# Differential attention on one Trainium2 core: the order of transposes, scores and sums on TensorE

## The chip, the core and the metric

The kernel runs on one core of a Trainium2 chip. The metric is the device time of one execution in microseconds (us), the median of several runs. The profile shows one execution: TensorE (PE; its weight loads are PEld), VectorE (DVE), ScalarE (ACT), GpSimd (POOL) and SyncE (SP, which issues transfers). The engines run side by side, each through its own instructions in the order of the program, and wait for each other by semaphores only.

## What is computed

Two transformer blocks one after the other, on 1024 tokens of width 1024. The change touches one stage of the second block, attention with two softmaxes per head: 4 heads, head width 64 for each of the two parts, values of width 128, 1024 queries and 1280 keys (256 of a context and the 1024 tokens). Cut to what matters:

```python
def diff_attend(q, k, v, lam):
    s = jnp.einsum('bqhmd,bkhmd->bhmqk', q, k, preferred_element_type=jnp.float32)
    a = jax.nn.softmax(s * (1.0 / math.sqrt(ATTN_HEAD_DIM)), axis=-1)
    a = a[:, :, 0] - lam * a[:, :, 1]
    return jnp.einsum('bhqk,bkhe->bqhe', a.astype(v.dtype), v)

def head_out(o, subln_g, lam_init):
    b, t = o.shape[:2]
    return (rmsnorm(o, subln_g) * (1.0 - lam_init)).reshape(b, t, ATTN_V_W)
```

The index m is the part (0 or 1). After this stage come the output projection and a mixture of experts, which take most of the rest of the kernel together with the same steps of the first block.

## The kernel before

The kernel is a chain of stages, each a block in which every engine has its own program and at whose end all meet. The stage here is `differential_attention` (line 2600). It goes through G = 32 groups: head h = g // 8, query tile t = g % 8 of 128 queries. All of TensorE's results go to 8 banks of PSUM, each of 128 partitions x 512 numbers. Banks 0 to 2 hold the scores of part 0 (128 queries x 1280 keys), banks 3 to 5 those of part 1, banks 6 and 7 the transposed probabilities, and bank 7 also the sums. For each group:

- `scores(g, i)` (line 2657, matmuls on lines 2672 and 2676): six matmuls for part i. They wait until ScalarE has read the part's scores of the group before (`exped[i]`).
- `bias(g, i)` on VectorE (line 2743, the reduction on 2746): the negated maximum of each row of scores.
- `exp(g, i)` on ScalarE (line 2792, on 2800): the exponentials with their row sums. The results lie in `e[g % 2]`.
- `combine(g)` on VectorE (line 2748; reciprocals on 2753 and 2755, the ratio on 2756, the combination on 2758): part 0 minus the scaled part 1, in place.
- `turn(g, r)` on TensorE (line 2680, transposes on 2692), three parts by r: the ten key tiles are turned so that keys lie on partitions. `GROUPS` gives the tiles of a part and `BANK` its bank. Part 0 (tiles 0 to 3, bank 6) waits for `combined`, part 1 (tiles 4 to 7, bank 7) for `kept`, part 2 (tiles 8 and 9, bank 6 again) for the first copy out of bank 6.
- `move(g, r)` on ScalarE (line 2803, on 2808): the copy of one part from its bank to `at_[g % 2]` in SBUF.
- `sums(g)` on TensorE (line 2696, matmuls on 2701): 20 recorded loads and matmuls against the values, into bank 7. They wait for all three copies of the group.
- `keep(g)` on VectorE (line 2761, on 2765): the sums times the reciprocal of part 0, out of bank 7. `square(g)` on ScalarE (2812) and `norm(g)` on GpSimd (2865) end the group.

The loops are written out by hand, and their order is fixed on each engine. VectorE, per g: `bias(g + 1, 0)`, `combine(g)`, `bias(g + 1, 1)`, `keep(g - 1)`. ScalarE, per g: `exp(g + 1, 0)`, `exp(g + 1, 1)`, `square(g - 2)`, the three moves of g. TensorE, per g (lines 2710 to 2719): `scores(g + 1, 1)`, `sums(g - 1)`, `turn(g, 0)`, `scores(g + 2, 0)`, `turn(g, 1)`, `turn(g, 2)`. GpSimd first splits the queries and keys of heads 1 to 3 into high and low parts (`split`, subtractions on lines 2852 and 2860), then normalizes group after group. SyncE issues four loads of 512 KB for the next stage. In the trace the scores' operands are called upper_split_qk, the probabilities arena, and the copies' targets arena or upper_tail.

Of the kernel before, what the change touches and what calls it, by code (L numbers as in the profile page):

```python
# [49 lines left out]
NK2 = SA // P  # L50
# [110 lines left out]
def rounded(ap):  # L161

    return ap.bitcast(F32R)
# [2434 lines left out]
def differential_attention(core, m):  # L2600
# [14 lines left out]
    combined, turned, moved, summed, kept, steps, gained, squared, normed, pool_steps = map(sem, (  # L2615
        "combined", "turned", "moved", "summed", "kept", "steps", "gained", "squared", "normed", "pool_steps"))
    e, at_ = m["e2"], m["a2"]
    at = m["free_too"]

    def take(*shape):  # L2620
        nonlocal at
        n = int(np.prod(shape))
        at += n
        return core.place(at - n, *shape)
# [1 line left out]
    G = NH2 * NT  # L2626
    nb, den, inv, ratio = take(4), take(4), take(4), take(4)
    gain, junk, ss, rs = take(P), take(P), take(G), take(G)
    GROUPS = ((0, 4), (4, 8), (8, NK2))
    BANK = (6, 7, 6)  # L2630
    FOLD = float(HD2) ** -0.5
    full = ps[:].rearrange("p a b -> p (a b)")
    rows = [full[:, 3 * i * HALF:3 * i * HALF + SA] for i in range(2)]
# [3 lines left out]
    with nc.Block() as block:  # L2637
        @block.sync
        def _(sp):
            for i in range(2):  # L2640
                sp.wait_ge(k_low[i], 1)
            sp.wait_ge(k_split[NH2 - 1], 2)
            for k in range(4):
                sp.dma_start(m["wo2"][k], core.ins["w_out2_k"][:, k, :]).then_inc(m["wo2_loaded"], 16)
            sp.wait_ge(m["wo2_loaded"], 16 * 4)

        @block.tensor
        def _(pe):
            def turn_v(h):
                i = (h + 1) % 2  # L2650
                if h >= 2:
                    pe.wait_ge(v_moved[h - 2], 2)
                for t in range(NK2):
                    ins = pe.transpose(rows[i][:, t * P:(t + 1) * P], v1[:, h, t * P:(t + 1) * P], core.col("ident"))
                ins.then_inc(v_turned[h], 1)

            def scores(g, i):
                h, t = where(g)
                x, cols = 2 * (h % HEADS) + i, slice(t * P, (t + 1) * P)
                if g:  # L2660
                    pe.wait_ge(exped[i], g)
                if t == 0:
                    if h == 0:
                        pe.wait_ge(v_moved[3 - i], 2)
                        pe.wait_ge(k_low[i], 1)
                        pe.wait_ge(q_copied[i], 2)
                    else:
                        pe.wait_ge(k_split[h], 2)
                        pe.wait_ge(q_split[h], 2)
                for c, wd in enumerate((HALF, HALF, CTX)):  # L2670
                    keys = slice(c * HALF, c * HALF + wd)
                    pe.matmul(ps[:, 3 * i + c, 0:wd], rounded(qa[:, x, cols]), rounded(ka[:, x, keys]),
                              start=True, stop=False, skip_group_check=True)
                for c, wd in enumerate((HALF, HALF, CTX)):
                    keys = slice(c * HALF, c * HALF + wd)
                    t = pe.matmul(ps[:, 3 * i + c, 0:wd], rounded(ql[:, x, cols]), rounded(ka[:, x, keys]),
                                  start=False, stop=True, skip_group_check=True)
                t.then_inc(scored[i], 1)

            def turn(g, r):  # L2680
                lo, hi = GROUPS[r]
                if r == 0:
                    pe.wait_ge(combined, g + 1)
                    if g:
                        pe.wait_ge(moved, 3 * g)
                elif r == 1:
                    if g:
                        pe.wait_ge(kept, g)
                else:
                    pe.wait_ge(moved, 3 * g + 1)  # L2690
                for t in range(lo, hi):
                    ins = pe.transpose(ps[:, BANK[r], (t - lo) * P:(t - lo + 1) * P],
                                       e[g % 2][:, 1, t * P:(t + 1) * P], core.col("ident"))
                ins.then_inc(turned, 1)

            def sums(g):
                h, _ = where(g)
                pe.wait_ge(moved, 3 * g + 3)
                for t in range(NK2):
                    own = at_[g % 2][t // 8]  # L2700
                    ins = pe.matmul(ps[:, 7, 0:P], own[:, t % 8, :], vt[t // 8][:, t % 8, h * P:(h + 1) * P],
                                    start=(t == 0), stop=(t == NK2 - 1), skip_group_check=True)
                ins.then_inc(summed, 1)

            for h in range(NH2):
                turn_v(h)
            scores(0, 0)
            scores(0, 1)
            scores(1, 0)
            for g in range(G):  # L2710
                if g + 1 < G:
                    scores(g + 1, 1)
                if g:
                    sums(g - 1)
                turn(g, 0)
                if g + 2 < G:
                    scores(g + 2, 0)
                turn(g, 1)
                turn(g, 2)
            sums(G - 1)  # L2720

        def move_v(eng, copy, h):
            i = (h + 1) % 2
            eng.wait_ge(v_turned[h], 1)
            for lo, hi, dst in ((0, 8, vt[0]), (8, NK2, vt[1])):
                copy(dst[:, :, h * P:(h + 1) * P],
                     rows[i][:, lo * P:hi * P].rearrange("p (a b) -> p a b", b=P)).then_inc(v_moved[h], 1)
# [57 lines left out]
        @block.scalar  # L2785
        def _(a):
            def high(i):
                a.activation(rounded(ka[here[i], i, :]), k[here[i], 0, :], ACT.Copy).then_inc(k_high[i], 1)
                a.activation(rounded(qa[here[i], i, :]), q[here[i], 0, :], ACT.Copy, scale=FOLD)\
                 .then_inc(q_high[i], 1)  # L2790

            def exp(g, i):
                x = 2 * (g % 2) + i
                a.wait_ge(biased[i], g + 1)
                if g >= 2:
                    if i == 0:
                        a.wait_ge(combined, g - 1)
                    else:
                        a.wait_ge(turned, 3 * (g - 1))
                a.activation(e[g % 2][:, i, :], rows[i], ACT.Exp, bias=nb[:, x:x + 1],  # L2800
                             accum_out=den[:, x:x + 1]).then_inc(exped[i], 1)

            def move(g, r):
                lo, hi = GROUPS[r]
                a.wait_ge(turned, 3 * g + r + 1)
                if g >= 2:
                    a.wait_ge(summed, g - 1)
                a.activation(at_[g % 2][r // 2][:, lo % 8:lo % 8 + hi - lo, :],
                             ps[:, BANK[r], 0:(hi - lo) * P].rearrange("p (a b) -> p a b", b=P), ACT.Copy)\
                 .then_inc(moved, 1)  # L2810

            def square(g):
                h, i = where(g)
                a.wait_ge(kept, g + 1)
                if g:
                    a.wait_ge(squared, g)
                a.activation(junk, o[:, h, i * P:(i + 1) * P], ACT.Square, accum_out=ss[:, g:g + 1])\
                 .then_inc(squared, 1)

            high(0)  # L2820
            high(1)
            copy = lambda dst, src: a.activation(dst, src, ACT.Copy)
            for h in (0, 2, 3):
                move_v(a, copy, h)
            exp(0, 0)
            exp(0, 1)
            for g in range(G):
                if g + 1 < G:
                    exp(g + 1, 0)
                    exp(g + 1, 1)  # L2830
                if g >= 2:
                    square(g - 2)
                for r in range(3):
                    move(g, r)
            square(G - 2)
            square(G - 1)
# [723 lines left out]
def build(nc, ins, out):  # L3560

    with ExitStack() as ctx:
# [150 lines left out]
        with ExitStack() as kind:  # L3713
# [18 lines left out]
        m["wo2_loaded"], m["wo2_rest"], m["rows_loaded"] = map(core.semaphore, (  # L3732
            "wo2_loaded", "wo2_rest", "rows_loaded"))
        run(differential_attention, m)
        kind.close()
        del core.regions[tail]
# [154 lines left out]
```

## Time and profile before

| | before |
|---|---|
| runs, us | 3062.36, 3063.38, 3066.44 |
| median, us | 3063.38 |
| the profiled execution, us | 3064.91 |
| its span in the profile, us | 3062.8 |
| granted TensorE clock, mean | 0.97 |
| TensorE matmul, busy us (share of the span) | 2854.3 (93%) |
| VectorE, busy us | 2088.0 (68%) |
| ScalarE, busy us | 1580.2 (52%) |
| GpSimd, busy us | 491.6 (16%) |

The profile is one execution on the core. All times in it are us from the start of the span unless marked ns. PE busy is the time in which a matmul was in flight; since matmuls overlap, the starts of the weight loads (PEld) show better when TensorE went on to the next. A row of the timeline merges like instructions that follow on one another; what stands in brackets is how long the engine was idle before it, and who released it. The clock is given as a share of full speed: 1.00 is 2.4 GHz and 0.50 is 1.2 GHz.

### The profile page before, as it was taken

What the parts mean: (1) busy time and instruction counts of PE and PEld (TensorE: products, weight loads), DVE (VectorE), ACT (ScalarE), POOL (GpSimd) and SP (SyncE); (2) the same over time, 40 slices, a digit from 0 to 9 for tenths busy, and PEclk for the clock granted to TensorE, in tenths of its full rate; (3) what the DMA queues carried; (4) which work ended last, traced back from release to release, by engine and by line L of the source; (5) the groups of instructions that cost most, each with busy time, mean ns of one, the idle gap of its engine ahead of it and who ended that gap; (6) DMA issues with size and microseconds to landing.
All of it is one profiled execution on the core that took longest, in us unless ns stands there. A gap on an engine that the chain in (4) does not pass through costs nothing. (4 is left out here: it accounts for less than half of the span.)

```text
span 3062.8 us, 38625 instructions
## 1 busy us (share of the span) xinstructions
PE 2854.3 (93%) x14112; PEld 2295.7 (75%) x14112; DVE 2088.0 (68%) x2213; ACT 1580.2 (52%) x1951; POOL 491.6 (16%) x501
## 2 busy tenths in 40 slices
PE   6998998999999999999998989998989579999998
PEld 4884466788877778888886878887877468888886
DVE  6988454332327788888886743317866679999997
ACT  4111565532212277787785531116663168887885
POOL 0004500000000011111112312009643100000001
PEclk9998999999999999999999999999999789999999
DMA  7112332643227476996215511100005669999997
GB/s 274 48 34 76 121 87 67 186 154 144 97 83 282 164 277 246 407 413 236 92 58 206 177 59 51 52 14 24 6 1 200 241 256 409 408 400 399 398 396 264
DMA packets 144569, 574.68 MB, mean 188 GB/s; under 512 B 18520, under 2 KB 41840, under 8 KB 104496
## 3 DMA queue, kind: packets, MB, share of 16 engines
q1 hardware_dynamic: 116560, 486.05, 41.8%
q0 software_dynamic: 15696, 57.15, 5.6%
q10 hardware_dynamic: 12176, 29.63, 2.7%
q8 instruction: 88, 1.44, 0.2%
q14 instruction: 49, 0.40, 0.0%
HBM read 584.99 MB, written 82.17 MB: 218 GB/s over the span
## 5 line engine op out<-in xcount | busy, mean ns | idle before, releaser
L2023 DVE TENSOR_TENSOR upper_split<-arena,upper_split 128x2048 fp32r<-128x2048 f32 x185 | 413.0, 2285 | 67.4 <-ACT upper_split L1970 65.7
L3505 DVE TENSOR_TENSOR upper_split_experts<-arena,upper_split_experts 128x1024 fp32r<-128x1024 f32 x288 | 337.6, 1221 | 33.5 <-ACT upper_split_experts L3449 33.4
L1970 ACT ACTIVATE upper_split<-arena 128x2048 fp32r<-128x2048 f32 x184 | 339.5, 1911 | 7.5 <-PE banks L177 6.6
L3449 ACT ACTIVATE upper_split_experts<-arena 128x1024 fp32r<-128x1024 f32 x288 | 288.5, 1053 | 83.9 <-PE banks L177 83.9
L175 PE MATMUL banks<-upper_split_experts 128*128 128x512 f32 x768 | 303.2, 395 | 6.1 <-DVE upper_split_experts L3505 3.6
L175 PE MATMUL banks<-upper_split 128*128 128x512 f32 x744 | 297.4, 400 | 4.5 <-PEq L1622 2.1
L177 PE MATMUL banks<-upper_split_experts 128*128 128x512 f32 x768 | 300.5, 391 | 0.0
L176 PE MATMUL banks<-upper_split_experts 128*128 128x512 f32 x768 | 300.0, 391 | 0.0
L177 PE MATMUL banks<-upper_split 128*128 128x512 f32 x744 | 291.7, 392 | 0.0
L176 PE MATMUL banks<-upper_split 128*128 128x512 f32 x744 | 291.0, 391 | 0.0
L175 PEld LDWEIGHTS banks<-upper_split_experts 128*128 128x128 f32 x768 | 145.1, 189 | 35.9 <-issue 4.0
L175 PE MATMUL banks<-upper_split_xn 128*128 128x512 f32 (+1 forms) x448 | 169.7, 379 | 2.3 <-DVE upper_split_xn L2306 1.6
L176 PE MATMUL banks<-upper_split_xn 128*128 128x512 f32 (+1 forms) x448 | 169.2, 378 | 0.0
L177 PE MATMUL banks<-upper_split_xn 128*128 128x512 f32 (+1 forms) x448 | 168.5, 376 | 0.0
L177 PEld LDWEIGHTS banks<-upper_split_experts 128*128 128x128 f32 x768 | 144.8, 189 | 30.6
L176 PEld LDWEIGHTS banks<-upper_split_experts 128*128 128x128 f32 x768 | 145.2, 189 | 29.4
L175 PEld LDWEIGHTS banks<-upper_split 128*128 128x128 f32 x744 | 140.4, 189 | 33.1 <-issue 3.3
L177 PEld LDWEIGHTS banks<-upper_split 128*128 128x128 f32 x744 | 140.5, 189 | 30.7
L176 PEld LDWEIGHTS banks<-upper_split 128*128 128x128 f32 x744 | 140.7, 189 | 27.9
L249 DVE SCALAR_TENSOR_TENSOR arena<-arena 128x1024 f32<-128x1024 f32 x120 | 153.7, 1322 | 1.7
L1296 DVE TENSOR_TENSOR upper_latent<-upper_latent,arena 128x512 f32<-128x512 f32 x48 | 33.3, 693 | 175.7 <-ACT upper_latent L1248 175.7
L175 PE MATMUL banks<-upper_split_h,upper_split_gates 128*128 128x512 f32 x384 | 149.5, 389 | 1.1 <-DVE upper_split_gates L1268 1.1
(486 smaller groups left out, 6308.2 us busy)
## 6 DMA issues: line engine op xcount, KB each, us to landing
arena<-in_exp_up_k SPq DMA_DIRECT2D x124, 1024.0 KB
arena<-in_gate_up SPq DMA_DIRECT2D x96, 1024.0 KB, 9.1
arena<-in_exp_down_k SPq DMA_DIRECT2D x62, 1024.0 KB
arena<-in_down SPq DMA_DIRECT2D x48, 1024.0 KB, 8.0
upper_middle<-in_gate_up SPq DMA_DIRECT2D x32, 1024.0 KB, 8.6
upper_middle<-in_down SPq DMA_DIRECT2D x16, 1024.0 KB, 8.1
y<-arena POOLq DMA_DIRECT2D x31, 512.0 KB, 4.1
arena<-in_merge_w SPq DMA_DIRECT2D x8, 1536.0 KB, 10.3
```

The lines of the kernel that those rows point to most:

```text
L175: pe.matmul(out, rounded(lh), rounded(rh), start=first, stop=False, skip_group_check=True)
L176: pe.matmul(out, rounded(lh), rounded(rl), start=False, stop=False, skip_group_check=True)
L177: return pe.matmul(out, rounded(ll), rounded(rh), start=False, stop=last, skip_group_check=True)
L249: t = v.scalar_tensor_tensor(acc, src, weight, acc, ALU.mult, ALU.add)
L1296: v.tensor_tensor(part[min(b, 1)], sg[done % 4], y[t % 2][:, b, here], ALU.mult).then_inc(steps, 1)
L1970: a.activation(rounded(high[s]), raw[s], ACT.Copy).then_inc(high_made[up], 1)
L2023: v.tensor_tensor(rounded(low[s]), raw[s], plain(high[s]), ALU.subtract).then_inc(low_made[up], 1)
L3449: a.activation(rounded(high[n % RING][:, half]), raw[n % RAW][:, half], ACT.Copy).then_inc(high_made, 1)
L3505: v.tensor_tensor(rounded(low[n % RING][:, half]), raw[n % RAW][:, half], plain(high[n % RING][:, half]), ALU.subtract).then_inc(low_made, 1)
```

## The change

`sums(g - 1)` is placed behind `turn(g, 0)` and `scores(g + 2, 0)`. The transposes of tiles 8 and 9 come second, into bank 6, with the wait for the first copy out of it. Those of tiles 4 to 7 come third, into bank 7, with the wait for `kept`. ScalarE's copies follow the new order of the parts, and each tile goes to the same place in SBUF as before. VectorE's and GpSimd's programs are as they were.

```diff
--- before.py
+++ after.py
@@ -2626,8 +2626,8 @@
     G = NH2 * NT
     nb, den, inv, ratio = take(4), take(4), take(4), take(4)
     gain, junk, ss, rs = take(P), take(P), take(G), take(G)
-    GROUPS = ((0, 4), (4, 8), (8, NK2))
-    BANK = (6, 7, 6)
+    GROUPS = ((0, 4), (8, NK2), (4, 8))
+    BANK = (6, 6, 7)
     FOLD = float(HD2) ** -0.5
     full = ps[:].rearrange("p a b -> p (a b)")
     rows = [full[:, 3 * i * HALF:3 * i * HALF + SA] for i in range(2)]
@@ -2684,10 +2684,9 @@
                     if g:
                         pe.wait_ge(moved, 3 * g)
                 elif r == 1:
-                    if g:
-                        pe.wait_ge(kept, g)
-                else:
                     pe.wait_ge(moved, 3 * g + 1)
+                elif g:
+                    pe.wait_ge(kept, g)
                 for t in range(lo, hi):
                     ins = pe.transpose(ps[:, BANK[r], (t - lo) * P:(t - lo + 1) * P],
                                        e[g % 2][:, 1, t * P:(t + 1) * P], core.col("ident"))
@@ -2710,11 +2709,11 @@
             for g in range(G):
                 if g + 1 < G:
                     scores(g + 1, 1)
-                if g:
-                    sums(g - 1)
                 turn(g, 0)
                 if g + 2 < G:
                     scores(g + 2, 0)
+                if g:
+                    sums(g - 1)
                 turn(g, 1)
                 turn(g, 2)
             sums(G - 1)
@@ -2805,7 +2804,7 @@
                 a.wait_ge(turned, 3 * g + r + 1)
                 if g >= 2:
                     a.wait_ge(summed, g - 1)
-                a.activation(at_[g % 2][r // 2][:, lo % 8:lo % 8 + hi - lo, :],
+                a.activation(at_[g % 2][lo // 8][:, lo % 8:lo % 8 + hi - lo, :],
                              ps[:, BANK[r], 0:(hi - lo) * P].rearrange("p (a b) -> p a b", b=P), ACT.Copy)\
                  .then_inc(moved, 1)
```

## Rows read from the trace of the kernel before

**Rows 1.** The page, part 1: busy us, share of the span, instructions.

```profile
PE 2854.3 (93%) x14112; PEld 2295.7 (75%) x14112; DVE 2088.0 (68%) x2213; ACT 1580.2 (52%) x1951; POOL 491.6 (16%) x501
```

**Rows 2.** Table by stretch, the stage whole; the first line names the columns.

```profile
core 0: us, PE busy (x) PEld busy (x) DVE busy (x) ACT busy (x) POOL busy (x), PEclk, DMA share, GB/s
...
2076.92:2294.24 217.32, 193.56 (x1344) 173.02 (x1344) 169.68 (x224) 142.72 (x287) 148.99 (x163) 0.98 0.03 11
```

**Rows 3.** Timeline, weight loads, two groups: start, us, engine, line, operation [idle before].

```profile
2189.97 1.87 PEld L2701 LDWEIGHTS banks<-upper_middle,upper_tail 128*128 128x128 f32 x16
...
2192.65 0.54 PEld L2672 LDWEIGHTS banks<-upper_split_qk 128*128 128x128 f32 x3
...
2193.82 0.47 PEld L2692 LDWEIGHTS banks<-arena 128*128 128x128 f32 x4
...
2195.58 0.20 PEld L2692 LDWEIGHTS banks<-arena 128*128 128x128 f32 x2 [1.28 <-ACT arena L2808]
...
2196.91 1.87 PEld L2701 LDWEIGHTS banks<-upper_middle,arena 128*128 128x128 f32 x16
...
2199.15 0.47 PEld L2692 LDWEIGHTS banks<-arena 128*128 128x128 f32 x4
...
2202.66 1.43 PEld L2701 LDWEIGHTS banks<-upper_middle,upper_tail 128*128 128x128 f32 x12
```

**Rows 4.** Timeline, ScalarE, the same two groups.

```profile
2193.34 1.33 ACT L2800 ACTIVATE arena<-banks,upper_tail 128x1280 f32<-128x1280 f32 x1 [2.01 <-DVE upper_tail L2746]
...
2194.95 1.07 ACT L2808 ACTIVATE arena<-banks 128x512 f32<-128x512 f32 x2
```

**Rows 5.** Timeline, VectorE, the same two groups.

```profile
2194.14 1.49 DVE L2746 TENSOR_REDUCE upper_tail<-banks 128x1 f32<-128x1280 f32 x1 [0.58 <-PE banks L2676]
...
2195.54 0.15 DVE L2753 RECIPROCAL upper_tail<-upper_tail 128x1 f32<-128x1 f32 x1
...
2196.10 1.55 DVE L2758 SCALAR_TENSOR_TENSOR arena<-arena,upper_tail 128x1280 f32<-128x1280 f32 x1
...
2199.46 0.35 DVE L2765 TENSOR_SCALAR arena<-banks,upper_tail 128x128 f32<-128x128 f32 x1 [0.41 <-PE banks L2701]
```

**Rows 6.** Timeline, weight loads and VectorE, first and last groups of the stage.

```profile
2092.31 1.87 PEld L2701 LDWEIGHTS banks<-upper_middle,arena 128*128 128x128 f32 x16
...
2092.78 2.30 DVE L2758 SCALAR_TENSOR_TENSOR arena<-arena,upper_tail 128x1280 f32<-128x1280 f32 x1
...
2095.13 0.42 PEld L2692 LDWEIGHTS banks<-arena 128*128 128x128 f32 x4 [0.51 <-DVE arena L2758]
...
2095.52 0.53 PEld L2672 LDWEIGHTS banks<-upper_split_qk 128*128 128x128 f32 x3
...
2273.01 1.87 PEld L2701 LDWEIGHTS banks<-upper_middle,arena 128*128 128x128 f32 x16
...
2293.89 0.35 DVE L2765 TENSOR_SCALAR arena<-banks,upper_tail 128x128 f32<-128x128 f32 x1 [4.21 <-PE banks L2701]
```

**Rows 7.** Groups by line in the stage; count | busy us, mean ns; then one line (min/median/max).

```profile
L2758 DVE SCALAR_TENSOR_TENSOR arena<-arena,upper_tail 128x1280 f32<-128x1280 f32 x32 | 54.4, 1699 | 1.1
...
L2852 POOL TENSOR_TENSOR upper_split_qk<-arena,upper_split_qk 64x1280 fp32r<-64x1280 f32 x6 | 17.5, 2922 | 0.5
...
L2758 DVE SCALAR_TENSOR_TENSOR arena<-arena,upper_tail x32: 1550/1553/2355, 2086.0 to 2284.1; 128x1280 f32<-128x1280 f32 x32
```

**Rows 8.** Timeline, GpSimd, the end of its splitting.

```profile
2152.53 2.18 POOL L2843 CAST upper_split_qk<-upper_split_qk 64x1024 fp32r<-64x1024 f32 x1
```

**Rows 9.** Table by stretch, columns as in rows 2, start of the stage.

```profile
2083.65:2087.07 3.42, 1.66 (x8) 0.98 (x6) 3.04 (x5) 1.77 (x4) 3.33 (x2) 1.00 0.00 0
...
2087.07:2090.48 3.41, 2.84 (x10) 2.45 (x11) 1.91 (x2) 1.46 (x3) 3.20 (x4) 0.50 0.00 0
```

**Rows 10.** Timeline, weight loads, start of the stage.

```profile
2082.46 0.53 PEld L2672 LDWEIGHTS banks<-upper_split_qk 128*128 128x128 f32 x3 [1.76 <-ACT arena L2800]
...
2087.64 0.71 PEld L2692 LDWEIGHTS banks<-arena 128*128 128x128 f32 x4 [2.47 <-DVE arena L2758]
```

## The prediction, made before the changed kernel was run

> **What bounds the kernel now.** I read the page first: TensorE is busy for 93% of the whole span [rows 1], so on average it is the bound, and an average says nothing of one stage. The stretch table of the stage that the diff touches (first score to last sum, 217.3 us) shows 193.6 us of TensorE and 169.7 us of VectorE [rows 2]: neither is full. The stage treats 32 groups. Its timeline repeats every two of them: the sums of group 15 start at 2189.97, those of group 17 at 2202.66, so a pair takes 12.69 us and a group 6.35 [rows 3].
>
> In one pair TensorE idles once for long: 1.28 us at 2195.58, ahead of the last two transposes, until ScalarE has copied the first four out of bank 6 [rows 3]. That copy (2194.95, two copies in the row) was late because it stands behind both exponentials [rows 4]. Everything else on TensorE is back to back: without that wait a group is (12.69 - 1.28) / 2 = 5.70 us. Of these the sums take 2.24 (2196.91 to 2199.15) and each of the two score blocks 1.17 (2192.65 to 2193.82) [rows 3], which leaves 1.12 for the ten transposes, 0.11 each. VectorE waits too, 0.58 us for scores and 0.41 for sums in the rows shown [rows 5]. So it has slack as the orders stand now.
>
> **Part by part.** All instructions stay, so nothing is removed or added. Moved are (a) `sums(g - 1)`, 20 matmuls, behind `turn(g, 0)` and `scores(g + 2, 0)`; (b) the two transposes of key tiles 8 and 9 to second place; (c) the four of tiles 4 to 7 to bank 7 and last place, behind the wait for `kept`; ScalarE's copies follow the same order. No DMA and no SyncE or GpSimd instruction is moved or passed.
>
> (b) The two transposes still need the first copy out of bank 6, but now 2.24 us of sums stand ahead of that wait. In the new order that copy ends before the sums do (worked out below), so the 1.28 us per pair go.
>
> (c) The last four transposes wait for `keep(g - 1)`, which now follows directly on the sums. From the first load of the sums to the start of `keep` it takes 2.55 us (2196.91 to 2199.46), `keep` itself 0.35 [rows 3, 5]; with 0.04 for the signal (an estimate, next to the 0.05 below) they can start 2.94 after the sums did, and TensorE has work for 2.24 + 0.22. That is 0.48 us idle in each group. Taken alone, a group would be 6.18 us, slightly under the 6.35 of now.
>
> (a) is what decides. VectorE's program is not changed: per group `bias(g+1, 0)`, `combine(g)`, `bias(g+1, 1)`, `keep(g-1)`, in that order, and it cannot pass a waiting `keep`. Behind `keep(g-1)` are queued `bias(g+2, 0)` and `combine(g+1)`. On TensorE, `sums(g)` now stands behind `turn(g+1, 0)`, which waits for `combine(g+1)`, and behind `scores(g+3, 0)`. So the sums of one group wait, through five instructions of VectorE, for the sums of the group before. Today this ring does not exist: sums stand ahead of the transposes that wait for `combine`. The ring, step by step:
> - sums, first load to start of `keep`: 2.55 [rows 3, 5]
> - `keep`: 0.35 [rows 5]
> - `bias` to the first reciprocal: 1.40 (2194.14 to 2195.54) [rows 5]
> - reciprocals and ratio to the start of the combination: 0.56 (to 2196.10) [rows 5]
> - the combination: 1.55 [rows 5]
> - signal to TensorE 0.05 (2092.78 + 2.30 = 2095.08, transposes at 2095.13) and four transposes 0.39 (to 2095.52) [rows 6]
> - the score block: 1.17 [rows 3]
>
> Sum 8.02 us a group against 6.35. Checking who else could be later, counted from the start of the sums: the combination before ended at -(1.17 + 0.39 + 0.05) = -1.61; `bias(g+1, 1)` follows and takes 1.5 (the row at 2194.14) [rows 5], from the start of its exponential to that of the first copy are 1.61 (2193.34 to 2194.95) [rows 4], the copy is 0.6, so it ends at about 2.1, under 2.24; the other score block runs from 3.4 to 4.5; TensorE then idles until 6.45, about 1.9 us. The ring is the longest chain and VectorE and TensorE wait in turn: about 2.3 us of 8.02 TensorE is idle.
>
> Entry: `sums(0)` starts at 2092.31 now [rows 6]. After the change it waits for the combination of group 1, which ends at 2095.08 either way, then 0.05 + 0.39 + 1.17: 2096.69, that is +4.4. Middle: from `sums(0)` to `sums(28)` (2273.01) are 28 groups, 180.7 us now [rows 6]; then 28 x 8.02 = 224.6, +43.9. Exit: the last three groups have no further scores to serve and take 21.2 us now (2273.01 to 2294.24) [rows 6]; the waits there are only exchanged, so 0, between -1.7 and +1.7.
>
> One term is not in 8.02. While GpSimd splits keys and queries the combination takes longer: 1699 ns in the mean of 32 against 1550, 4.8 us in all, longest 2355 [rows 5, 7]. 0.75 of it is in the entry. The splitting ends at 2154.7 [rows 8]; about 9 groups of now share the other 4.0, about 7 of the new ones lie in the same time, and now each such delay is on the ring: +3.2, between 0 (GpSimd out of step) and 7 x 0.80 = 5.6.
>
> Sum: 4.4 + 43.9 + 3.2 = +51.5. For the clock (next part) I add 1.7, one slow stretch, against 0 to 7: +53.2. The profiled execution is 3062.8 us and 3064.9 with what lies around it; its run is 1.5 above the median of the three. So 3064.9 + 53.2 - 1.5 = 3116.6; I say 3117.
>
> **Rivals.**
> *The clock falls.* TensorE works 5.7 of 8.0 us with a gap of 1.9 in each group. In this trace it idled 1.76 us and went on at full rate, and after 2.47 us four weight loads took 0.71, not the 0.42 of 2095.13 [rows 6, 10]; the clock granted around that gap fell from full to half (2.4 to 1.2 GHz) for 3.4 us, after a stretch with 1.66 us of work in 3.42 [rows 9]. The new gap is nearer to the first. A combination of 2.3 us makes it 2.7. A slow stretch of 3.4 us on the ring costs at most half, 1.7: four of them in GpSimd's part +7, one in every group +48, 3164.
>
> *The combination is blocked for whole instructions.* Rows: GpSimd's subtraction takes 2922 ns, and no combination is more than 0.80 us longer than its shortest [rows 7]. If each of the 7 waited a whole one, that is +20 in place of 3.2: 3133. The Trainium skill, "SBUF — State Buffer", section "SBUF: two separate sides", says so: one of GpSimd and a VectorE operation with two SBUF inputs holds the shared ports to its end. By that rule the time would be 3133; the trace shows 0.80 at most, so I trust it little.
>
> *Not slower: TensorE sets the pace.* If VectorE's order did not close the ring, a group would be 6.18 us: 28 x 6.18 = 173.0, +4.4 entry, 3.3 less than now: 3060. With (c)'s wait hidden as well, 5.70 a group, 16.7 less: 3047. It decides from the point at which `bias(g+2, 0)` can start before `keep(g-1)`: its scores are done some 2.2 us before `keep`. VectorE would have to serve them out of order; in the rows each `keep` stands where the program has it, at 2199.46 after a wait of 0.41 [rows 5].
>
> **How the numbers follow.** Forecast (ring, few slow stretches) 0.76; clock beyond 7 us 0.14; blocked combinations 0.03; TensorE's pace 0.04 (3060 and 3047, half each); the rest, a mis-sized term beyond the bounds, 0.03. The forecast's own bounds: -1.7 exit, -3.2 combinations, -1.7 clock, -2.5 if `keep` hands over at 0.26: 3107. Upward 2.4 + 5.3 + 1.7 and 0.1 a group (2.8): 3129. To leave out no more than 2 in 10 the range goes on into the clock's case: 3107 to 3135. A measurement can tell about 0.2% (6 us) from no change. Faster 0.02, same 0.02, slower 0.96.
>
> **What would show it.** In the profile after: sums 8.0 us apart in every group, no more pairs; VectorE waiting for the sums ahead of `keep` about 2.9 us, and not for scores ahead of the first `bias`; TensorE waiting for the combination about 1.9 us ahead of the first transposes and for `keep` about 0.5; no wait for the first copy; all other stages unchanged. I am wrong if sums stand 6.2 apart (no ring), or if the granted clock of the stage falls well below 0.98.

## The result, and the profile after

| | before | after |
|---|---|---|
| median of the runs, us | 3063.72 (4 runs, 3062.36 to 3066.44) | 3114.96 (4 runs, 3114.60 to 3116.24) |
| ratio to before | | 1.0168 (1.0157 to 1.0180) |
| profiled execution, us | 3064.91 | 3116.24 |
| its span, us | 3062.8 | 3114.3 |
| the stage, first score to end of the last `keep`, us | 217.3 | 269.7 |
| TensorE busy in the stage, us | 193.6 | 203.3 |
| VectorE busy in the stage, us | 169.7 | 168.5 |
| a group in the quiet part of the stage, us | 6.35 | 7.92 |

The change costs 51.2 us, 1.7%. The prediction was 3117, with 3107 to 3135 as the range. The span is 51.5 us longer, and the stage ends 51.5 us later (2345.78 in place of 2294.24), so all of it is in the stage. (The first score came 0.9 us earlier, at 2076.05 in place of 2076.92; counted from there the stage is 52.4 longer.) The stretch table of after, over the stage and over one group:

```profile
core 0: us, PE busy (x) PEld busy (x) DVE busy (x) ACT busy (x) POOL busy (x), PEclk, DMA share, GB/s
2076.05:2345.80 269.75, 203.29 (x1344) 174.19 (x1344) 168.50 (x224) 148.15 (x287) 134.16 (x164) 0.97 0.02 9
2199.62:2207.54 7.92, 6.08 (x44) 5.23 (x43) 5.10 (x7) 4.60 (x10) 1.81 (x4) 1.00 0.00 0
```

To be read against rows 2: 52 us more, of which VectorE has none and TensorE 10. Both wait more. What one group looks like now stands in the timeline of TensorE's weight loads (line 2691 holds the transposes, 2700 the sums):

```profile
2198.07 0.42 PEld L2691 LDWEIGHTS banks<-arena 128*128 128x128 f32 x4 [1.93 <-DVE arena L2757]
...
2199.62 1.87 PEld L2700 LDWEIGHTS banks<-upper_middle,arena 128*128 128x128 f32 x16
...
2201.41 0.53 PEld L2700 LDWEIGHTS banks<-arena,upper_tail 128*128 128x128 f32 x4
...
2201.85 0.25 PEld L2691 LDWEIGHTS banks<-arena 128*128 128x128 f32 x2
...
2202.57 0.42 PEld L2691 LDWEIGHTS banks<-arena 128*128 128x128 f32 x4 [0.46 <-DVE arena L2764]
...
2202.96 0.53 PEld L2672 LDWEIGHTS banks<-upper_split_qk 128*128 128x128 f32 x3
...
2205.99 0.42 PEld L2691 LDWEIGHTS banks<-arena 128*128 128x128 f32 x4 [1.93 <-DVE arena L2757]
...
2206.38 0.53 PEld L2672 LDWEIGHTS banks<-upper_split_qk 128*128 128x128 f32 x3
...
2207.54 1.87 PEld L2700 LDWEIGHTS banks<-upper_middle,upper_tail 128*128 128x128 f32 x16
```

From one start of the sums (2199.62) to the next (2207.54) are 7.92 us, in every group alike; the pairs of [rows 3] are gone. TensorE waits twice: 1.93 us for the combination ahead of the first four transposes, and 0.46 for `keep` ahead of the last four. It no longer waits for the first copy out of bank 6: the two transposes at 2201.85 follow the sums at once. VectorE in the same group (2745 the reduction, 2757 the combination, 2764 `keep`):

```profile
2202.17 0.35 DVE L2764 TENSOR_SCALAR arena<-banks,upper_tail 128x128 f32<-128x128 f32 x1 [2.75 <-PE banks L2700]
2202.43 1.48 DVE L2745 TENSOR_REDUCE upper_tail<-banks 128x1 f32<-128x1280 f32 x1
2203.83 0.15 DVE L2752 RECIPROCAL upper_tail<-upper_tail 128x1 f32<-128x1 f32 x1
2204.39 1.55 DVE L2757 SCALAR_TENSOR_TENSOR arena<-arena,upper_tail 128x1280 f32<-128x1280 f32 x1
2205.86 1.48 DVE L2745 TENSOR_REDUCE upper_tail<-banks 128x1 f32<-128x1280 f32 x1
```

VectorE stands idle for 2.75 us ahead of `keep`, and from then on nothing of the ring waits: `keep`, the reduction of the scores that had long been ready, the reciprocal, the combination; then TensorE's transposes at 2205.99, scores and sums. In [rows 5] `keep` waited 0.41 and the reduction 0.58 for scores; in the other group of the pair the reduction waited 1.26. Over the whole stage VectorE now waits 92.8 us for the sums. The two ends of the middle part (first sums, the 29th sums, the last `keep`), which answer to [rows 6]:

```profile
2096.49 1.87 PEld L2700 LDWEIGHTS banks<-upper_middle,arena 128*128 128x128 f32 x16
...
2326.29 1.87 PEld L2700 LDWEIGHTS banks<-upper_middle,arena 128*128 128x128 f32 x16
...
2345.43 0.35 DVE L2764 TENSOR_SCALAR arena<-banks,upper_tail 128x128 f32<-128x128 f32 x1 [3.94 <-PE banks L2700]
```

### The profile page after: what moved, and what is told of

It reads as the page before. It is cut to its first block and busy times, and to the rows that moved or that the text cites. A ratio compares the mean times of both kernels' runs of the same rounds, so it can differ in the third digit from the quotient of the medians.

```text
span 3114.3 us, 38625 instructions
## 1 busy us (share of the span) xinstructions
PE 2862.0 (92%) x14112; PEld 2297.3 (74%) x14112; DVE 2088.0 (67%) x2213; ACT 1586.0 (51%) x1951; POOL 476.0 (15%) x501
## 5 line engine op out<-in xcount | busy, mean ns | idle before, releaser
L175 PE MATMUL banks<-upper_split_xn 128*128 128x512 f32 (+1 forms) x448 | 169.7, 379 | 2.3 <-DVE upper_split_xn L2306 1.6
```

Of the source, the lines that this page charges most:

```text
L175: pe.matmul(out, rounded(lh), rounded(rh), start=first, stop=False, skip_group_check=True)
```

## Experiments

All kernels ran with the kernel before on the same chip; medians of before were between 3061.8 and 3063.7. "A group" is the distance from one start of the sums to the next in the quiet part of the stage, behind GpSimd's splitting.

| kernel | median, us | ratio to before (interval) | a group, us |
|---|---|---|---|
| after | 3114.96 | 1.0168 (1.0157 to 1.0180) | 7.92 |
| e3_sums_moved, part (a) alone | 3114.67 | 1.0162 (1.0145 to 1.0179) | 7.92 |
| e2_order_of_parts, (b) and (c) alone | 3071.53 | 1.0026 (1.0017 to 1.0036) | 6.56 |
| e4_sums_half_way | 3110.25 | 1.0151 (1.0134 to 1.0168) | 7.67 |
| e1_bias_first | 3078.48 | 1.0043 (1.0031 to 1.0056) | 6.77 |
| e5_second_reduction | 3121.45 | 1.0192 (1.0177 to 1.0207) | 8.18 |
| e11_no_gain | 3116.99 | 1.0171 (1.0154 to 1.0189) | 7.92 |
| e7_no_split | 3106.98 | 1.0137 (1.0122 to 1.0152) | 7.92 |
| e8_copy_between | 3055.79 | 0.9978 (0.9968 to 0.9987) | 6.09 |
| e9_square_last | 3058.34 | 0.9980 (0.9972 to 0.9989) | 6.10 |

The theory is the prediction's: a ring through six instructions of VectorE (`keep`, the reduction, two reciprocals, the ratio, the combination) and three steps of TensorE (four transposes, a score block, the sums), closed by part (a). The rivals are that the new order of the parts carries the loss, that the amount of work on VectorE does, or that TensorE has its own reasons.

### Which part of the change does it

Part (a) alone, on the kernel before:

```diff
-                if g:
-                    sums(g - 1)
                 turn(g, 0)
                 if g + 2 < G:
                     scores(g + 2, 0)
+                if g:
+                    sums(g - 1)
```

> Part (a) alone: the sums behind the first transposes and the scores, the parts and banks as before. Ring theory: the ring is closed by (a) alone, and the waits of (b) and (c) lie inside TensorE's 2.3 us of slack: 7.92 us a group, 3115 within 2 us of the changed kernel. Rival that (b) and (c) carry a part: between 3064 and 3110.

Measured 3114.67 and 7.92 us a group. The parts keep their old order here, and the waits look different inside the group (timeline of the weight loads; 2701 are the sums, 2692 transposes):

```profile
2198.37 1.87 PEld L2701 LDWEIGHTS banks<-upper_middle,arena 128*128 128x128 f32 x16
...
2201.32 0.64 PEld L2692 LDWEIGHTS banks<-arena 128*128 128x128 f32 x6 [0.64 <-DVE arena L2765]
...
2204.74 0.42 PEld L2692 LDWEIGHTS banks<-arena 128*128 128x128 f32 x4 [1.71 <-DVE arena L2758]
...
2206.28 1.87 PEld L2701 LDWEIGHTS banks<-upper_middle,upper_tail 128*128 128x128 f32 x16
```

Six transposes wait 0.64 us for `keep`, the first four 1.71 for the combination, and the distance of the sums is the same 7.92. How the slack is cut up makes no difference; (a) is the whole loss.

Parts (b) and (c) alone are the changed kernel with the sums put back ahead of `turn(g, 0)`:

> Parts (b) and (c) alone: the sums stand where they stood before, the two transposes of tiles 8 and 9 come second into bank 6, the four of tiles 4 to 7 last into bank 7. Ring theory: no ring, since the sums are ahead of the transposes that wait for the combination; the wait for the first copy out of bank 6 stays and has 0.45 us of transposes less ahead of it, only in every second group: up to 0.2 us a group more than before, 3064 to 3071. Rival that the new order of the parts (the wait for keep) carries the loss: 3080 or more.

Measured 3071.5, 8.6 us above the kernel before and half a microsecond above the range that was expected; that only every second group would be longer did not come true. Groups of 6.87 and 6.25 us take turns, 13.12 a pair against 12.69: 0.21 us a group more. The wait for the first copy is now there in both groups of a pair (0.70 and 1.32 us), since the four transposes that used to stand ahead of it stand behind it. So (b) and (c) are a small loss by themselves, which the ring hides once it is closed.

### Does the ring have the members that the prediction gave it?

The sums moved by half the way, behind the transposes but ahead of the scores:

```diff
                 turn(g, 0)
-                if g + 2 < G:
-                    scores(g + 2, 0)
                 if g:
                     sums(g - 1)
+                if g + 2 < G:
+                    scores(g + 2, 0)
```

> The changed kernel with the sums moved past the first transposes only; scores(g+2, 0) stand behind the sums again. Ring theory: the ring now runs sums 2.24, score block with its last results 1.17 + 0.32, reduction 1.40, reciprocals and ratio 0.56, combination 1.55, signal 0.05, four transposes 0.39 = 7.68 us a group, 0.24 less than 7.92: 28 x 0.24 = 6.7 less, about 3108. Rival that the scores between transposes and sums are simply 1.17 us of the ring that leave it: 6.75 a group, 3082. Rival without a ring: 3064.

```profile
2200.98 0.42 PEld L2691 LDWEIGHTS banks<-arena 128*128 128x128 f32 x4 [2.12 <-DVE arena L2757]
...
2201.37 1.86 PEld L2700 LDWEIGHTS banks<-upper_middle,arena 128*128 128x128 f32 x16
...
2208.65 0.42 PEld L2691 LDWEIGHTS banks<-arena 128*128 128x128 f32 x4 [2.12 <-DVE arena L2757]
...
2209.04 1.87 PEld L2700 LDWEIGHTS banks<-upper_middle,upper_tail 128*128 128x128 f32 x16
```

Measured 7.67 a group (2201.37 to 2209.04) where 7.68 was worked out, and 3110.25 where 3108 was. The score block did not leave the ring by changing places with the sums. It took the place of `keep`: the reduction now waits for it (0.82 us, behind a `keep` that is done).

One edit on VectorE alone, the reduction ahead of `keep`:

```diff
             bias(0, 1)
+            bias(1, 0)
             for g in range(G):
-                if g + 1 < G:
-                    bias(g + 1, 0)
                 combine(g)
                 if g + 1 < G:
                     bias(g + 1, 1)
+                if g + 2 < G:
+                    bias(g + 2, 0)
                 if g:
                     keep(g - 1)
```

> The changed kernel with one edit on VectorE alone: bias(g+2, 0) stands ahead of keep(g-1), not behind it. Ring theory: the 1.40 us of that reduction leave the ring, the combination stays on it, since it is still queued behind keep: 7.92 - 1.40 + 0.13 (the combination waits for the end of keep, 0.35, not for its hand-over, 0.26, and 0.04 of signal) = 6.65 us a group, so 1.27 x 28 = 35.6 us less than the changed kernel and one slow clock stretch fewer: about 3078, still slower than before. TensorE's-pace theory (the ring was only the reduction, as the rival in the prediction had it): 6.18 a group, about 3061. Rival that VectorE's order has nothing to do with it (the sums are late for TensorE's own sake): unchanged, 3115.

```profile
2199.68 0.42 PEld L2691 LDWEIGHTS banks<-arena 128*128 128x128 f32 x4 [0.78 <-DVE arena L2757]
...
2201.22 1.87 PEld L2700 LDWEIGHTS banks<-upper_middle,upper_tail 128*128 128x128 f32 x16
...
2204.16 0.42 PEld L2691 LDWEIGHTS banks<-arena 128*128 128x128 f32 x4 [0.47 <-DVE arena L2764]
...
2206.46 0.42 PEld L2691 LDWEIGHTS banks<-arena 128*128 128x128 f32 x4 [0.80 <-DVE arena L2757]
...
2208.00 1.87 PEld L2700 LDWEIGHTS banks<-upper_middle,arena 128*128 128x128 f32 x16
```

Measured 6.77 us a group (2201.22 to 2208.00; 6.65 expected) and 3078.5 (3078 expected). Ahead of the first transposes 0.80 us of wait are left of 1.93. 36 of the 51 us come back without touching TensorE. About 32 of them are the shorter ring (28 x 1.15); the stretch from `sums(0)` to `sums(28)` is 39.1 us shorter in the profile, which has no half-clock stretch there. The 0.12 beyond the expectation: the combination takes 1.62 us beside GpSimd, not 1.55, and the first reciprocal starts 0.46 after `keep`, not 0.39. The prediction's rival had it that without that reduction the ring would be open and a group 6.18. It is not: the combination is still behind `keep`, and the shorter ring still sets the pace. The program's order is not the only thing that holds it there: `combine(g + 1)` overwrites the reciprocals that `keep(g - 1)` reads, and waits for `kept`.

### Is it the work of VectorE, or its place?

The changed kernel with a second, unused reduction where VectorE waits for the sums:

```diff
                 v.wait_ge(scored[i], g + 1)
+                if i and g >= 2:
+                    v.tensor_reduce(spare, rows[i], AX, ALU.max, negate=True)
                 v.tensor_reduce(nb[:, x:x + 1], rows[i], AX, ALU.max, negate=True).then_inc(biased[i], 1)
```

> The changed kernel with work added on VectorE off the ring: the reduction of bias(g+1, 1) is done twice from group 2 on (once into an unused column), 1.40 us more of VectorE in 30 groups, 42 us in all. It stands between the combination and keep, where VectorE waits 2.75 us in each group. Ring theory: it fills that wait; the second exponential and the first copy come 1.4 later, the two transposes then wait until about 3.5 after the start of the sums instead of 2.2, but TensorE had slack until 6.4: 7.92 us a group, 3115 within 3 us. Rival that VectorE's work is what costs the time: 3157.

Measured 3121.45: far from 3157, but 6.5 us above the changed kernel and outside the 3 us given. A group took 8.18. GpSimd and VectorE in one group (2872 and 2873 are the last two steps of GpSimd's normalization, 2760 the combination, 2747 the added reduction, 2767 `keep`):

```profile
2205.97 0.61 POOL L2872 TENSOR_SCALAR arena<-arena,upper_tail 128x128 f32<-128x128 f32 x1
...
2206.66 0.47 POOL L2873 TENSOR_TENSOR arena<-arena,upper_tail 128x128 f32<-128x128 f32 x1
...
2206.65 1.82 DVE L2760 SCALAR_TENSOR_TENSOR arena<-arena,upper_tail 128x1280 f32<-128x1280 f32 x1
...
2208.39 1.48 DVE L2747 TENSOR_REDUCE upper_tail<-banks 128x1 f32<-128x1280 f32 x1
...
2212.61 0.35 DVE L2767 TENSOR_SCALAR arena<-banks,upper_tail 128x128 f32<-128x128 f32 x1 [1.35 <-PE banks L2701]
```

VectorE still waits 1.35 us ahead of `keep` (the added 1.40 came out of the 2.75), so the reduction is not what lengthens the group. The combination takes 1.82 us, not 1.55, in all quiet groups (1810 ns in the median of the 32), and it starts with GpSimd's multiplication by the gain, 2206.65 beside 2206.66. The squares start 1.40 us later in the group than in the changed kernel, and GpSimd's multiplication with them (4.78 after the start of the sums in place of 3.36): onto the combination. That was an observation from one profile, so the next kernel takes the multiplication away:

```diff
-                c.step(g.tensor_scalar(row, row, r, None, ALU.mult))
-                g.tensor_tensor(row, row, gain, ALU.mult).then_inc(normed, 1)
+                g.tensor_scalar(row, row, r, None, ALU.mult).then_inc(normed, 1)
```

> As e5_second_reduction, with GpSimd's last step of each group, the multiplication with the gain (0.47 us, it reads two operands out of SBUF), left out; so the gain is missing from the heads' output. In e5_second_reduction a group took 8.18 us, not 7.92, and each combination 1.81, not 1.55; it started 0.01 us before or after that multiplication. Theory that the combination waited for the end of the multiplication: with it gone the combinations take 1.55 again and a group 7.92, in spite of the second reduction: about 7 us less than e5_second_reduction, 3114. Rival that the added reduction itself lengthens the ring by 0.26: 8.18 a group stays, 3121.

```profile
2209.89 0.61 POOL L2872 TENSOR_SCALAR arena<-arena,upper_tail 128x128 f32<-128x128 f32 x1
2210.58 1.55 DVE L2760 SCALAR_TENSOR_TENSOR arena<-arena,upper_tail 128x1280 f32<-128x1280 f32 x1
```

The combination takes 1.55 us again and a group 7.92, with the second reduction in place. The median fell to 3117.0, 4.5 us less than with the multiplication where 7 were expected (its runs spread from 3112.2 to 3119.6). The times alone would not decide it: the profiled execution of e11_no_gain is the longer of the two, 3119.6 against 3117.8; the 7.92 a group does. 1.40 us of VectorE work in a group are free at this place, and 0.27 us on the ring are not.

Only in the last three groups, where no scores are left to do, does the added reduction cost time. TensorE waits 2.32 us there for the first copy in place of 0.93, and the clock is granted at half behind that wait; from `sums(28)` to the end of the stage are 22.5 us in e5_second_reduction and 23.3 in e11_no_gain, against 19.5.

### What lies between 7.92 a group and the time

28 groups of 7.92 are 221.8 us; from `sums(0)` to `sums(28)` the changed kernel took 229.8. The other 8.0 us lie in groups ahead of 2192, while GpSimd splits or catches up. The longest of these groups took 10.65 us; GpSimd, VectorE and TensorE in it:

```profile
2144.12 2.89 POOL L2851 TENSOR_TENSOR upper_split_qk<-arena,upper_split_qk 64x1280 fp32r<-64x1280 f32 x1
...
2144.98 3.38 DVE L2757 SCALAR_TENSOR_TENSOR arena<-arena,upper_tail 128x1280 f32<-128x1280 f32 x1
...
2147.10 3.89 POOL L2854 TENSOR_SCALAR arena<-arena 128x1024 f32<-128x1024 f32 x1
...
2148.41 0.42 PEld L2691 LDWEIGHTS banks<-arena 128*128 128x128 f32 x4 [3.76 <-DVE arena L2757]
```

The combination starts at 2144.98 and takes 3.38 us: GpSimd's subtraction runs to 2147.01, and from there to 2148.36 are 1.35 us, most of a combination. The 1.82 us in e5_second_reduction end as far behind the multiplication: 2207.13 to 2208.47. GpSimd's next step, 2.77 us in the kernel before, takes 3.89 and overlaps the rest. The wait of the one for the other is inside the recorded duration, not in the idle time. TensorE waited 3.76 us for it. The three stretches in which the clock was granted at half (1.2 GHz) within the middle part:

```profile
2104.47:2107.88 3.41, 3.41 (x17) 3.32 (x16) 0.02 (x1) 2.19 (x5) 3.27 (x3) 0.50 0.00 0
2121.53:2124.95 3.42, 3.42 (x15) 3.03 (x14) 1.07 (x1) 2.19 (x5) 3.28 (x3) 0.50 0.00 0
2148.84:2152.25 3.41, 3.41 (x15) 3.02 (x13) 0.92 (x1) 2.19 (x5) 3.28 (x3) 0.50 0.99 401
```

Each came after a gap on TensorE that was longer than the usual 1.93: 2.21, 2.58 and 3.76 us. Not every such gap brought one: after 2.42 us at 2094.95 and 2.20 at 2190.16 the rate stayed full. The middle one:

```profile
2121.25 0.46 PEld L2691 LDWEIGHTS banks<-arena 128*128 128x128 f32 x4 [2.58 <-DVE arena L2757]
2121.70 0.98 PEld L2672 LDWEIGHTS banks<-upper_split_qk 128*128 128x128 f32 x3
```

Three weight loads of a score block take 0.98 us in place of 0.53. In the 17 groups from 2191.70 to 2326.29, with a gap of 1.93 us each and 0.46 more, the full rate was not taken back once. In the middle part six combinations are longer than 1.6 us, by 3.3 us in all, which leaves, by difference, 4.7 for the three stretches, 1.6 each. Whether both come from GpSimd is what the next kernel asks; `split(h)` and the waits for it are left out.

> The changed kernel with GpSimd's splitting of keys and queries for heads 1 to 3 left out: all heads are scored with head 0's operands, so part of the computation is changed; GpSimd only normalizes. Theory (GpSimd in the way of the combinations, and the clock stretches that follow from it, make up all of the time beyond 7.92 a group): 28 groups at 7.92, 8.0 us less in the middle and 0.6 less ahead of it, no half-clock stretch between the first and the last sums: 3106. Theory of the prediction (3.2 us by the combinations, at most 0.80 each, the clock apart from that): 3110, the slow clock stretches staying. Rival that the long groups have another cause: 3115.

Measured 3106.98, and every group from the first to the 29th sums took 7.91 to 7.93 us, without a half-clock stretch among them. All of the 8.0 us hang on GpSimd's splitting and the catching up behind it: directly through the ring, and through the clock. How they divide between the two no run shows; both went together.

### Is the wait for the first copy what holds the kernel before back?

On the kernel before, ScalarE alone:

```diff
                 if g + 1 < G:
                     exp(g + 1, 0)
+                move(g, 0)
+                if g + 1 < G:
                     exp(g + 1, 1)
                 if g >= 2:
                     square(g - 2)
-                for r in range(3):
+                for r in range(1, 3):
                     move(g, r)
```

> The kernel before with one edit on ScalarE alone: the first copy of a group, move(g, 0), stands between exp(g+1, 0) and exp(g+1, 1), not behind both. If the 1.28 us that TensorE waits for this copy in every second group is all that holds the kernel before back, as the prediction said: the copy is taken at about 2.8 after the start of the sums in every group, the two transposes find bank 6 free, and a group takes between 5.70 (TensorE alone) and 6.0 (the second exponential starts up to 0.4 later, and the score block waits for it) instead of 6.35: 10 to 18 us less, 3046 to 3053. Rival that the wait is exchanged for another one: 3063.

ScalarE (2800 the exponential, 2808 the copies) and TensorE's loads:

```profile
2198.44 1.32 ACT L2800 ACTIVATE arena<-banks,upper_tail 128x1280 f32<-128x1280 f32 x1
...
2200.03 0.60 ACT L2808 ACTIVATE arena<-banks 128x512 f32<-128x512 f32 x1
...
2194.97 1.87 PEld L2701 LDWEIGHTS banks<-upper_middle,upper_tail 128*128 128x128 f32 x16
...
2198.80 0.69 PEld L2692 LDWEIGHTS banks<-arena 128*128 128x128 f32 x6
...
2199.90 0.53 PEld L2672 LDWEIGHTS banks<-upper_split_qk 128*128 128x128 f32 x3 [0.41 <-ACT arena L2800]
...
2201.05 1.87 PEld L2701 LDWEIGHTS banks<-upper_middle,arena 128*128 128x128 f32 x16
```

Measured 3055.8, ratio 0.9978 (0.9968 to 0.9987): faster than both kernels, though less than the 10 us expected. Six transposes go through in one run at 2198.80. In their place the next score block waits 0.41 us for the second exponential, in every group: 6.09 us a group in place of 6.35. The median is 7.7 us lower (the interval of the ratio allows 4 to 10). In the profiles 4.6 of it lie between `sums(0)` and `sums(28)` (176.1 in place of 180.7 us): 0.26 in each of the last 18 groups, while the first ten took 66.5 us in both kernels. There the long combinations add up to 9.5 us in place of 4.7, the longest 4.28. The rest of the 7.7 is not placed. The expectation had a group at 6.0 at most.

> As e8_copy_between, and the square of group g-2 behind the last copy, not ahead of the second. The other two copies come 0.3 us earlier. Theory that the second score block now waits only for the second exponential: same as e8_copy_between within 2 us; theory that the copies ahead of the sums set the pace: 0.3 us a group less, about 8 us less than it. Either way under 3055.

With the squares behind the last copy: 3058.3, ratio 0.9980 (0.9972 to 0.9989), 6.10 a group. Both kernels were expected under 3055 and are not, and the median is 2.5 us above e8_copy_between, but the intervals of the two overlap and the groups are alike. Copies that come earlier gain nothing: the copies behind the second exponential do not set the pace there.

## Why the prediction was right, point by point

- **The ring.** It closed as described, on (a) alone, and lasts 7.92 us where 8.02 was worked out. The 0.10 is the hand-over from `keep` to the reduction: 0.26 us (2202.17 to 2202.43), not the full 0.35, which stood as the lower bound. 28 x 0.10 = 2.8 us less. The prediction counted five instructions of VectorE; with both reciprocals they are six, and all their time is in the sum.
- **Entry.** `sums(0)` at 2096.49, 4.2 us later than before; 4.4 was said. Part of the agreement is luck, since the first score came 0.9 us earlier: from it to `sums(0)` are 20.4 us in place of 15.4.
- **Middle.** 229.8 us; 224.6 + 3.2 + 1.7 = 229.5 was said. The agreement is partly luck: the ring was 2.8 too long, and the clock was too small, three slow stretches (4.7) and not one (1.7).
- **GpSimd.** 3.3 us of longer combinations against 3.2. The sum held, by luck in part, since one combination makes 1.83 of it; the bound did not: "no combination is more than 0.80 us longer" was true of one profile of before. The Trainium skill, "SBUF — State Buffer", section "SBUF: two separate sides", has the two engines exclude each other for a whole instruction when VectorE reads two operands from SBUF and GpSimd reads SBUF too. The 3.38 us above and e11_no_gain agree with it, and the prediction was wrong to trust it little. What did not follow is the rival's price: few combinations meet the start of a long instruction, so the sum was 3.3 and not 20. The trace of before already spoke for whole instructions. The longest combination there:

```profile
2129.67 2.91 POOL L2852 TENSOR_TENSOR upper_split_qk<-arena,upper_split_qk 64x1280 fp32r<-64x1280 f32 x1
...
2131.57 2.35 DVE L2758 SCALAR_TENSOR_TENSOR arena<-arena,upper_tail 128x1280 f32<-128x1280 f32 x1
```

It ends 1.34 us behind the end of the subtraction (2132.58 to 2133.92). So do, by 1.34 to 1.36, seven of the nine long combinations in the middle part of before and five of the six in that of the changed kernel; the other three stand beside a multiplication by a scalar (2855, in the changed kernel 2869) and end sooner. The 0.80 was what was left of an instruction that had started 1.90 us earlier, and no bound.

- **Exit.** 19.5 us (2326.29 to 2345.78) against 21.2: -1.7, the lower bound; 0 was said. Not only the waits changed: the kernel before had a half-clock stretch here (2285.02 to 2288.44, PEclk 0.50), and the changed kernel none. The 16 loads of a group's sums took 3.36 us in it, where the changed kernel takes 1.86:

```profile
2285.29 3.36 PEld L2701 LDWEIGHTS banks<-upper_middle,arena 128*128 128x128 f32 x16 [0.71 <-ACT upper_tail L2808]
```

- **(b) and (c).** The 1.28 us per pair went, 0.48 (measured 0.46) came in each group, and neither mattered, since TensorE had 1.93 us of further slack.
- **The clock.** The rival in which it falls in every group did not come true. With a gap of 1.93 in each group it stayed at full rate. The term itself was too small: one stretch (1.7) was allowed for, three came in the middle and one went at the exit.
- **The rival that TensorE sets the pace** was to decide itself "from the point at which `bias(g+2, 0)` can start before `keep(g-1)`". e1_bias_first shows that this point was wrong: the reduction ahead of `keep` is not enough, a group is then 6.77 and not 6.18, because the combination stays in the ring.

Open is why before, e2_order_of_parts and e8_copy_between fall into their particular patterns while GpSimd is splitting; only the changed kernel was run without the splitting.

## What to carry to other kernels

Moving work later on one engine is only free if nothing that follows it on another engine is needed for what it was moved behind; write down the ring (who waits for whom, through every in-order queue) before and after, and add up its members. A ring sets its pace with every engine partly idle, so busy shares do not show it, and work added where the ring waits costs nothing as long as the ring sets the pace. Where a wait sits on one engine, the cheapest cure may be the order on another: here one line of ScalarE gave what the change on TensorE was after.

## What the hardware showed that had not been expected

- A VectorE combination with two operands in SBUF waited out GpSimd instructions: 3.38 us for 1.55 beside a subtraction of 2.89, and 4.28 in e8_copy_between; even a multiplication of 0.47 us cost 0.27 in each quiet group of e5_second_reduction. The waiting is recorded as duration, so it does not appear among the idle times. Behind subtractions, casts and this multiplication the combination ended 1.34 to 1.36 us after GpSimd's instruction had ended, however long that was.
- TensorE's clock stayed at full rate through 17 groups on end with gaps of 1.93 and 0.46 us in 7.92 (28 groups in e7_no_split; 20 in e4_sums_half_way with one gap of 2.12 in 7.67), and fell to half after gaps of 2.21, 2.58 and 3.76, but not after 2.42 and 2.20 elsewhere in the same stage: the length of one gap alone did not decide it.
